# Preparing a two-way recurrence and closing a feed-forward block: loads, buffers and a product in passes

## The reference

```
dec   = exp(-exp(-0.5) * sigmoid(w0[d] + tanh(wd[d]) @ w2[d]))
a     = sigmoid(a0[d] + ad[d] @ a2[d]);   g = sigmoid(gd) @ g2
kk    = k * k_k;  kk = kk / max(sqrt(sum over the head of kk*kk), 1e-12)
kd[d] = k * (1 + (a - 1) * k_a)
step:  S = S*dec + (S @ -kk) (kk*a)^T + v kd^T;   y = S @ r
```

```
h   = silu(x3 @ W_gate) * (x3 @ W_up)          # 1024 tokens x 2816
y   = 2**0.25 * x3 + h @ W_down                # W_down 2816 x 1024
out = (y - mean(y)) / sqrt(var(y) + 1e-5) * ln2_w + ln2_b     # over the 1024 columns
```

## Time and profile before

| | |
|---|---|
| median of 3 runs | 4634.16 us |
| the profiled execution, its own time | 4633.02 us |
| its span in the trace | 4630.9 us |
| PE, DVE, ACT busy | 81%, 55%, 33% |
| stage `rp` | 2928 to 3117 us |
| stage `fd` | 4318 to 4572 us |
| stage `l2` | 4572 us to the end |

### The profile page before, as it was taken

The page is one execution under the profiler, slowest core; times in us unless marked ns, Lnnn a source line. Parts: engine busy times, 40 slices in busy tenths (PEclk is TensorE's granted clock), DMA queues, the critical chain, the costliest instruction groups (busy, mean ns, idle before and its releaser), DMA issues. The chain is left out here.

```text
span 4630.9 us, 62673 instructions
## 1 busy us (share of the span) xinstructions
PE 3765.7 (81%) x25680; PEld 3091.3 (67%) x25680; DVE 2524.6 (55%) x2755; ACT 1519.5 (33%) x1842; POOL 89.8 (2%) x57
## 2 busy tenths in 40 slices
PE   6999958989499999399993655329998788999994
PEld 5888847768377777278882344109995667888783
DVE  5673327966288888644414879555555442111235
ACT  3222114545077777311121232333332231111233
POOL 0000000000100000100000010000000000000002
PEclk8999979989599999699996777659998999999997
DMA  6422217455499999632221131451110432111113
GB/s 236 182 96 91 91 51 217 153 205 182 165 397 398 399 398 380 240 116 89 99 77 63 48 133 57 132 135 41 56 40 20 147 114 64 51 46 46 46 64 145
DMA packets 354606, 661.30 MB, mean 143 GB/s; under 512 B 54152, under 2 KB 150168, under 8 KB 352186
## 3 DMA queue, kind: packets, MB, share of 16 engines
q1 hardware_dynamic: 318890, 536.92, 34.0%
q10 hardware_dynamic: 24688, 79.17, 4.3%
q0 software_dynamic: 10784, 41.70, 2.2%
HBM read 506.01 MB, written 163.26 MB: 145 GB/s over the span
## 5 line engine op out<-in xcount | busy, mean ns | idle before, releaser
L156 PE MATMUL fu_ps<-x3T_hi,fu_w_lo 128*128 128x512 f32 x704 | 275.2, 391 | 9.0 <-DVE fu_w_lo L3103 9.0
L156 PE MATMUL g_ps<-x2T_hi,g_w_lo 128*128 128x512 f32 x704 | 275.0, 391 | 8.9 <-DVE g_w_lo L339 8.9
L157 PE MATMUL fu_ps<-x3T_lo,fu_w_hi 128*128 128x512 f32 x704 | 274.8, 390 | 0.0
L158 PE MATMUL fu_ps<-x3T_hi,fu_w_hi 128*128 128x512 f32 x704 | 274.8, 390 | 0.0
L157 PE MATMUL g_ps<-x2T_lo,g_w_hi 128*128 128x512 f32 x704 | 274.8, 390 | 0.0
L158 PE MATMUL g_ps<-x2T_hi,g_w_hi 128*128 128x512 f32 x704 | 274.6, 390 | 0.0
L383 DVE COPY g_st<-g_ps 128x512 f32<-128x512 f32 x40 | 27.7, 692 | 323.2 <-PE g_ps L158 323.2
L1498 DVE TENSOR_TENSOR moe_wg_lo<-moe_wg,moe_wg_hi 128x2048 fp32r<-128x2048 f32 x68 | 155.7, 2292 | 68.7 <-ACT moe_wg_hi L1452 68.7
L371 DVE SCALAR_TENSOR_TENSOR g_st<-g_pad,g_par,g_st 128x1024 f32<-128x1024 f32 x140 | 179.9, 1285 | 11.2 <-issue 0.9
L156 PE MATMUL g_ps<-h1T_hi,g_w_lo 128*128 128x512 f32 x448 | 175.2, 391 | 7.0 <-DVE g_w_lo L339 7.0
L3103 DVE TENSOR_TENSOR fu_w_lo<-fu_w,fu_w_hi 128x1024 fp32r<-128x1024 f32 x44 | 53.8, 1222 | 227.6 <-ACT fu_w_hi L3086 227.6
(11 more groups left out here) (611 smaller groups left out, 10097.6 us busy)
## 6 DMA issues: line engine op xcount, KB each, us to landing
moe_wg<-in_exp_w_gate SPq DMA_DIRECT2D x68, 1024.0 KB
moe_wu<-in_exp_w_up SPq DMA_DIRECT2D x68, 1024.0 KB
moe_wd<-in_exp_w_down SPq DMA_DIRECT2D x66, 1024.0 KB
g_w<-in_w_in SPq DMA_DIRECT2D x96, 512.0 KB, 4.2
go_w_raw<-in_w_out SPq DMA_DIRECT2D x64, 512.0 KB
s_conv<-g_st ACTq DMA_DIRECT2D x14, 2048.0 KB, 6.9
s_xs<-g_zero POOLq DMA_DIRECT2D x1, 24064.0 KB
s_ys<-moe_y ACTq DMA_DIRECT2D x47, 512.0 KB, 6.2
```

Of the source, the lines that this page charges most:

```text
L156: pe.matmul(out, l[1], r[0], start=(k == 0), stop=False)
L157: pe.matmul(out, l[0], r[1], start=False, stop=False)
L158: return pe.matmul(out, l[0], r[0], start=False, stop=(k == kt - 1))
```

## The change

In `rw_prepare`:

- the one semaphore `c_in` becomes `cols_in`, `w_in` and `sel_in`; each engine waits for what it reads, where it reads it;
- the loads are in a new order: `lr`, `cols`, part 0 of `k`, `bd`/`sel`/`selt`, parts 1 to 3 of `k`, `wt`, `r` 0 and 1, then `v`; `r` has two buffers in place of four, and `r` 2 and 3 are loaded after the stores of parts 0 and 1;
- `edge` is not loaded; DVE sets it by two memsets at the start;
- `vs` has two copies, used by turns, with a semaphore for each copy and direction: the waits for `stored` begin at part 2 and are for the part two before;
- `sq` uses `e3`'s memory, and `ks` uses `t1`'s, for which the wait for `sums` is moved ahead of `t1`.

At the end, `gemm_deep` and `residual_norm` are replaced by one `deep_norm` with three passes of 3, 3 and 2 tiles, 22 blocks each; `fo` isn't written.

```diff
-        vs, e3 = s.sb("vs", [P, 2, NRC, 4, RC]), s.sb("e3", [P, 2, SEQ])
+        vs, e3 = s.sb("vs", [P, 2, 2, NRC, 4, RC]), s.sb("e3", [P, 2, SEQ])
+        sq = e3
...
             sp.dma_start(lr[:, :, :], rows(conv[R0 + 3 * W:R0 + RW_COLS, :])).then_inc(lr_in, 16)
-            sp.dma_start(cols_t[:, :, :], cols).then_inc(c_in, 16)
-            for p in range(RP):
+            sp.dma_start(cols_t[:, :, :], cols).then_inc(cols_in, 16)
+            sp.dma_start(kT[:, 0], conv[R0 + W:R0 + W + P, :]).then_inc(k_in[0], 16)
+            for t, src in ((bd_t[:, :], bd), (sel_s[:, :, :], sel), (selt_s[:, :, :], sel_t)):
+                sp.dma_start(t, src).then_inc(sel_in, 16)
+            for p in range(1, RP):
                 sp.dma_start(kT[:, p], conv[R0 + W + p * P:R0 + W + p * P + P, :]).then_inc(k_in[p], 16)
...
+                if p + 2 < RP:
+                    load_r(p + 2)
...
-            pe.wait_ge(c_in, past(160))
+            pe.wait_ge(sel_in, past(48))
...
             pe.wait_ge(nl, past(2))
+            pe.wait_ge(w_in, past(80))
...
-            act.wait_ge(c_in, past(160))
             act.wait_ge(lr_in, past(16))
             act.activation(lr[:, 0], lr[:, 0], ACT.Tanh).then_inc(nl, 1)
             act.activation(lr[:, 2], lr[:, 2], ACT.Sigmoid).then_inc(nl, 1)
+            act.wait_ge(cols_in, past(16))
...
-                if p:
-                    act.wait_ge(stored[0], past(64 * p))
+                if p >= 2:
+                    act.wait_ge(stored[p % 2][0], past(64))
...
-            v.wait_ge(c_in, past(160))
+            v.memset(edge_t[:, :, :], 1.0)
+            v.drain()
+            v.memset(edge_t[:, :, 0:1], 0.0)
+            v.wait_ge(cols_in, past(16))
...
-                    if p:
-                        v.wait_ge(stored[d], past(64 * p))
+                    if p >= 2:
+                        v.wait_ge(stored[p % 2][d], past(64))
...
-        gemm_deep(nc, "fd", hid, A["ffn_w_down_2"], fo, n_out=2)
-    residual_norm(nc, "l2", x3, A["ln2_w_2"], C["ident"], None, alpha=DN_ALPHA, add=fo, bias=A["ln2_b_2"],
-                  eps=LN_EPS, y_out=out)
+        deep_norm(nc, "fd", hid, A["ffn_w_down_2"], x3, A["ln2_w_2"], out, ((0, 1, 2), (3, 4, 5), (6, 7)), alpha=DN_ALPHA,
+                  bias=A["ln2_b_2"], eps=LN_EPS, room=xT, n_r=5)
```

More of the change, by code:

```diff
@@ L2192, in rw_prepare @@
         p_g, p_r = s.ps("p_g", [P, SEQ]), s.ps("p_r", [P, SEQ])
-        c_in, lr_in = s.sem("c_in"), s.sem("lr_in")
+        cols_in, w_in, sel_in, lr_in = (s.sem(n) for n in ("cols_in", "w_in", "sel_in", "lr_in"))
         k_in, r_in, v_in = ([s.sem(f"{n}_in{p}") for p in range(RP)] for n in "krv")
-        stored = [s.sem(f"stored{d}") for d in range(2)]
+        stored = [[s.sem(f"stored{b}{d}") for d in range(2)] for b in range(2)]
         (nl, sq_ok, stat, root, inv, low_w, low_a, low_g, spread, sums, sg_ok, a_ok, g_ok, pad, c_ok, y_ok, m_ok, e1_ok, e2_ok,
@@ L2201, in rw_prepare, with parts @@
         block = s.block()
+        def parts(p):
+            return [vs[:, p % 2, :, :, k] for k in range(4)]
         def col(n, p):
@@ L2299, in _ @@
             for p in range(RP):
+                t2, kd, e2, e1 = parts(p)
                 act.wait_ge(low_w, past(p + 1))
@@ L2325, in _ @@
                 act.wait_ge(y_ok, past(p + 1))
-                if p:
-                    act.wait_ge(stored[1], past(64 * p))
+                if p >= 2:
+                    act.wait_ge(stored[p % 2][1], past(64))
                 act.activation(e2[:, 1], c[:, 1, :, 1:], ACT.Exp, scale=E05).then_inc(e2_ok, 1)
@@ L2364, in _ @@
                 v.scalar_tensor_tensor(kk[:, :], kT[:, p], col(0, p), p_r[:, :], ALU.mult, ALU.mult).then_inc(kk_ok, 1)
+                if p:
+                    v.wait_ge(sums, past(p))
                 v.drain()
@@ L3670, in second_layer @@
                    A["hy_skip_2"], A["c_hft"], spec, top)
-    x3, fo = (scratch(n, [SEQ, D]) for n in ("x3", "fo"))
+    x3 = scratch("x3", [SEQ, D])
     zh, zr = scratch("zh", [HY_W, SEQ]), scratch("zr", [RW_W, SEQ])
```

42 lines of the change are left out of this document (19 added, 23 removed).

## The result

The changed kernel takes 4555.87 us, the median of 4 runs (4550.01 to 4556.52), beside 4633.52 us for the kernel before on the same chip (4 runs, 4630.79 to 4634.8). The ratio is 0.983, with a 95% interval of 0.9813 to 0.9847. The forecast was 4557. The profiled execution took 4556.52 us with a span of 4554.7; its span is 76.2 us shorter than that of the one before (4630.9), and the sum had said 77.3.

A forecast was written before the change was run, and what follows sets the result against it. It took fd as bound by PE's matmuls, the final 56 us as uncovered norm work, and rp as held by DVE's waits. -10.5 - 26.6 - 64.0 + 15.8 + 8.6 - 0.6 = -77.3 us gave 4557; range 4550 to 4565, with rivals 4546 to 4576.

The forecast's parts named there:

- start of `rp` (first load to first scan): Start of stage rp: tanh waits only for cols, not all constants, and nothing takes the wait's place; -10.5 us.
- stores of `vs` (the rest of `rp`): Stage rp: with two copies of vs, all three DVE waits for stores go; -26.6 us.
- what stood behind the last matmul: End of program: drain, fo stores, stage change, loads and eight norms go, -64.0 us; a two-tile tail comes, +15.8 us.
- stalls of the last pass (PE's stretch): Last pass of fd: PE stalls 3.5 us behind ACT's squares and 5.1 us at DVE's scales; +8.6 us.
- first matmul of `fd` earlier: Start of fd: the low part of 384 hidden columns, not 1024, lies before the first matmul; -0.6 us.
- near 2945: Start of rp: estimated landing of wt, ending 4.4 MB of loads, ahead of PE's logits at 2950.
- the next bound: Stage rp: the store queue is late next, needing 22.5 us per part against DVE's 25.3, so SP keeps up.
- All at full clock: Last stage: expected sign that PE's matmuls keep full clock despite gaps in units 4 and 7 to 9.
- The rule weighed in the prediction: Last pass: waits between matmul bursts can bring back half clock; a 2.44 us gap in ow spoke against it.
- The rival of the half clock: Last pass: half clock returns behind the 3.5 us gap; time about 4563, at worst 4573; chance 0.08.
- weights didn't starve PE: Last stage: rival that weights, streamed three times, starve PE, making the kernel slower than before, 4703; chance 0.01.
- no half of the change failed to act: Either half: rival that the change doesn't act there, for instance stored still waited for in each part; 4584; chance 0.01.

The follow-up runs named there:

- e4: Changed kernel with PE and ACT first waiting for cols, sel and wt, in the new load order, edge still set on chip: 4565.11 us, ratio 0.9848.
- e5: Changed kernel with bd, sel and selt loaded last again, behind k and wt, each group keeping its own semaphore: 4561.58 us, ratio 0.9846.
- after: The changed kernel itself, with the new rw_prepare and deep_norm, against the kernel before: 4555.87 us, ratio 0.983.
- e3: Changed kernel with one copy of vs, so each part from 1 on waits for the stores of the part before: 4578.14 us, ratio 0.9874.
- e7: Changed kernel with deep_norm's centred squares one tile per unit, roots and variances with them, for the first two passes' tiles: 4552.85 us, ratio 0.9826.
- e6: Changed kernel with edge loaded by DMA behind wt on its own semaphore, in place of the two memsets: 4553.66 us, ratio 0.9827.
- e10: Changed kernel with four unused matmuls on PE ahead of unit 4 of the last pass, filling the 3.33 us gap: 4552.9 us, ratio 0.9829.
- e2: Kernel before with only the new last stage, deep_norm, and the old rw_prepare: 4592.23 us, ratio 0.9907.
- e1: Kernel before with only the new rw_prepare and the old last two stages: 4594.43 us, ratio 0.9914.
- e8: Changed kernel with all deep_norm work spread (sums, centring, squares, scales three units apart), stores two units behind the scales: 4553.86 us, ratio 0.9827.
- e11: The kernel with all norm work spread, its stores and the loads of r two units later in SP's program: 4544.69 us, ratio 0.9809.

## Why the prediction was right, by its own steps

| step | forecast | measured |
|---|---|---|
| start of `rp` (first load to first scan) | -10.5 | -12.7 |
| stores of `vs` (the rest of `rp`) | -26.6 | -27.5 |
| what stood behind the last matmul | -64.0 + 15.8 | -64.0 + 16.0 |
| stalls of the last pass (PE's stretch) | +8.6 | +9.7 |
| first matmul of `fd` earlier | -0.6 | -0.7 |
| elsewhere | 0 | +2.9 |
| span | -77.3 | -76.2 |

**The start** was right in mechanism (e4, e5) and under-sized by 2 us; two things were missing. I started the tanh where the table load of the earlier trace rows ends. In the earlier trace rows that table load waits for `lr`, and the tanh behind it for the constants; in after, where one wait is left, the table load runs at the stage's start, 2931.30, while `lr` is still on its way: 1.28 us. The tanh therefore starts 11.8 us earlier against its first load. The rest, 0.85 us, is ACT's last square of `k`, which waited 1.68 us for PE's sums before and 0.83 after. PE's 16 matmuls for these sums took 9.00 us in after and 9.86 before. The windows of after show PE's clock rising from 0.50 to 0.96 in 2946 to 2949, 4 to 7 us after its first matmul at 2942.23:

```profile
2943.00:2946.00 3.00, 3.00 (x5) 0.71 (x4) 0.00 (x0) 0.20 (x2) 0.00 (x0) 0.50 1.08 232
2946.00:2949.00 3.00, 3.00 (x8) 0.66 (x6) 0.00 (x0) 2.17 (x2) 0.00 (x0) 0.96 1.05 396
```

and of before, at 4 to 7 us after 2950.74, 0.76:

```profile
2955.00:2958.00 3.00, 3.00 (x7) 0.78 (x6) 0.00 (x0) 1.32 (x2) 0.00 (x0) 0.76 0.02 7
```

Why the clock rose sooner isn't shown, but it is no accident of one execution: the first scan comes 24.2 to 24.5 us after the first load in after and in the nine other programs with this start. The prediction's estimate that `wt` lands "near 2945" is 17 us after the first load at 2927.99, and e4 shows 17.2.

**The stores** gave all three waits, as e3 shows, and 0.9 us on top, which no run explains. What was foretold of the next bound holds: DVE's 25.3 us per part (24.99 and 25.34), the store queue in time. But the size was wrong. The stores of a part are 4 MB, not the 2 MB of the prediction (and 2 MB for each direction, not 1). The view of the transfers before, over all eight pairs of part and direction (count, KB each, median us to landing):

```profile
s_vecs<-rp_vs SPq DMA_DIRECT2D x8, 1024.0 KB, 8.0
s_vecs<-rp_vs SPq DMA_DIRECT2D x8, 512.0 KB, 9.2
s_vecs<-rp_vs SPq DMA_DIRECT2D x16, 256.0 KB, 9.3
```

The 23.3 us were measured and not reckoned from the size, so the forecast didn't suffer; but it means that the stores move at about 180 GB/s and not 90, and that the DMA engines, busy for 0.80 of the time in after, have less to spare than 2 MB would suggest.

**The tail** is the sum of small rows, 15.8 against 16.0. It is right because each term came from a row of the same shape, the scale by the minimum of the earlier trace rows, 0.81 us, which applies where POOL doesn't work.

**The stalls** came out right in sum and wrong in their parts. The first was to be 3.5 us and is 3.33, for the reason given, and e7 shows that the squares make it. The second was to be 5.1 and is 1.80. "All at full clock" failed: behind the 3.33 us gap the granted clock is 0.50, and 13 matmuls start 0.43 us apart and not 0.23, and behind the second gap another 8. That is about 4.4 us (21 spacings with some 0.2 us too much), so 5.1 + 4.4 + 0.2 of small idleness make 9.7.

The two falls didn't cost the same. Up to unit 9 the pass is 8.2 us late (32.7 against 24.5), in e3 to e6 as in after, and this is what the 8.6 of the forecast was for: ACT's squares and DVE's scales. The first fall cost nothing beside it, since DVE was the bound: while PE ran slowly, DVE caught up by as much as PE lost, and the second stall shrank from 5.1 to 1.80. e10 shows the exchange from the other side. The second fall, behind the last scale, met no other bound and cost its full 1.6 us; e2 to e6 don't have it, and the stretch of e3 to e6 is 249.6 to 249.7 us. So the mechanism of the stalls was right to 0.4 us, and the clock, which the sum left out, is the rest.

The rule weighed in the prediction (the Trainium skill, "TensorE: Matmul & The Clock Gate", section "HAM oscillation — how this bites in real kernels": waits between bursts of matmuls can bring the array back to half clock) agrees with this trace at the 3.33 us gap and at the 1.80 us gap behind it, and I had given the other side more weight because of the 2.44 us gap of the earlier trace rows. The rival of the half clock therefore had its mechanism right and its price, 4563 and more, wrong, because it added a loss that the stall beside it absorbs.

**The rivals** that didn't come: weights didn't starve PE in pass 1 and 2 (110.00 us of 110.00 busy, and no gap from PE's first matmul of `fd` to 4479.9 us), and no half of the change failed to act (e1, e2).

**Left open.** `rs` to `fu` and the time ahead of `rp` differ by 1 to 3 us from profile to profile in kernels that are the same there; the +2.9 in the table is of that size, and no run explains it. The cold start of `fd` lasts 7 to 13 matmuls in these profiles, and why, or why the clock falls behind one gap and not behind another of the same length, no run shows.

## What to carry to other kernels

A single semaphore for all constants makes each engine wait for the last of them; give each group its own and put the loads in the order in which they are first read, both together (12.8 us here; either alone leaves half or nothing). When norm work is hidden under a product's passes, count each engine's time per unit against PE's, put the heavy norm under the longest pass or spread it, and place every store in the queue's program at least as many units behind the work it waits for as the queue runs ahead (SP runs 3 ahead here; 2 behind stalled, 4 behind did not, 3 wasn't tried); a store placed early takes back nearly all that the spreading wins (e8 to e11: 9 us). And a loss on an engine that isn't the bound in that stretch isn't added to the sum, even if it is PE's clock.

## What the runs showed of the hardware

- The granted clock fell from 1.00 to 0.50 (2.4 to 1.2 GHz) behind the 3.33 us gap in every program that has it (after, e2, e3, e4, e5, e6), and 6 (e3) to 14 (e4, e6) matmuls ran slowly behind it. It fell behind some gaps of 1.80 to 2.06 us as well (after's second, e7's third, e8's second, e10's second), and not behind others of like length (e2's 2.03, e3's 2.07, e7's 1.81, e10's 1.99, e8's 1.66, and 1.65 to 1.70 us in e4 to e6), nor behind 1.31 and 2.44 us in the earlier trace rows.
- A fallen clock cost nothing while DVE was the bound (unit 9 starts at 32.6 to 32.7 us of the pass with none, 6 or 14 slow matmuls before it) and 1.6 us where nothing else was (after and e10 behind their last gap).
- A wait in SP's program holds every later DMA of that program. In e8, 23.0 us of such waits turned into 18.3 us of waits for weights on ACT and about 5.2 us of gaps on PE.
- A table load takes 1.28 us in each of these rows. In after it runs ahead of the wait for `lr` and costs nothing; in e4 it runs behind the wait for `wt`, and the tanh starts 1.30 us after that landing.
